# Strassen block products for 22 gate/up units of two feed-forward blocks

## The chip, the cores and the metric

The kernel runs on one core of one Trainium2 chip. It is timed in microseconds (us) of device time from start to end. Before the change three runs took 1771.74, 1771.89 and 1772.28 us; the median is 1771.89.

## What is computed

Three transformer-like blocks over 512 tokens and a model width of 1024 run one after the other: convolution mixer and feed-forward, dilated attention and feed-forward, and a third block with retention, sparse attention and a feed-forward with a small convolution. The change touches the first two feed-forwards and the additions around them:

```
def rmsnorm(x, g):
    y = x * rsqrt(mean(x * x, axis=-1) + EPS)
    return y * g

def swiglu(h, w_gate, w_up, w_down):
    return (silu(h @ w_gate) * (h @ w_up)) @ w_down      # 1024 -> 2816 -> 1024

h = rmsnorm(x, norm_ffn[i])
x = x + swiglu(h, ffn_w_gate[i], ffn_w_up[i], ffn_w_down[i])
```

## The kernel before

Everything is stored with channels on the 128 partitions and the 512 tokens as columns. A 1024-wide tensor is 8 such tiles. Weights come in **units**: a unit holds the weights of 256 output columns (two halves of 128) for all its input tiles, one half for the gate and one for the up projection in a gate/up unit. `LAYERS` (L24) lists the layers with their number of units and of input tiles: `pw2` 4 units of 8 tiles, `gu0a` 11 of 8, `dn0a` 4 of 11, `gu0b`, `dn0b`, `qkv` 9 of 8, `wo` 4 of 6, and for the second feed-forward `gu1a`, `dn1a`, `gu1b`, `dn1b`.

Each float32 product is made as three matmuls of rounded parts: weight high part by data high part, high by low, low by high (`product`, L640 to L648). A plain gate/up unit is therefore 2 halves x 8 tiles x 3 = 48 matmuls of 128x512. Weights arrive in `W_raw` (two buffers, SyncE's queue), ScalarE rounds them to `W_hi` (`split_hi`, `hi_of`, L1280 to L1294), and VectorE subtracts to get `W_lo` (`split_lo`, `lo_of`, L2059 to L2071). All three have two buffers, used in turn: the parts of unit u+2 can be written only when unit u is done (`acc_ready`), and unit u+2 can't begin before `w_lo` says that they are there (`unit`, L669).

Each engine has its own program, written out in order; nothing is rearranged by a scheduler. VectorE's part in a gate/up unit is `gate_steps` (L2221): scale both sums by the reciprocal root mean square R, multiply by the activated gate, then make the `W_lo` of the unit after next, then the low part of the hidden tile. In `pw2`, `wo` and the down layers it is `add_steps` (L2193): add the sums to X, make the normed low parts `H_lo` where a norm follows, then `W_lo`. ScalarE's programs of the same names (L1489, L1527) make `W_hi`, then `H_hi` and the squares for the norm. `R` enters only after the products, since it is a factor of each token.

Of the kernel before, what the change touches and what calls it, by code (L numbers as in the profile page):

```python
# [5 lines left out]
F32 = mybir.dt.float32  # L6
# [4 lines left out]
P = 128  # L11
# [17 lines left out]
          ("gu2a", 11, 8), ("dn2a", 4, 11), ("gu2b", 11, 8), ("dn2b", 4, 11)]  # L29

# [159 lines left out]
def build(nc, a, out):  # L190
# [6 lines left out]
    kts = [l.kt for l in order for _ in range(l.n)]  # L197
# [6 lines left out]
    with ctx:  # L204
# [25 lines left out]
        R = sb("R", [P, SEQ])  # L230
        STD = sb("STD", [P, SEQ])
# [17 lines left out]

        PADDED = SEQ + CONV_WIDTH - 1 + 2  # L250
# [17 lines left out]
        PT1 = [sb(f"PT1{i}", [P, SEQ], at=w_at + 11264 * i + 8192) for i in range(6)]  # L268
# [72 lines left out]
        ident, ones, swap, dup, dupswap, headsum = (cmat[:, i, :] for i in range(6))  # L341
        sel = [cmat[0:GROUP_HEADS, 6 + i, :] for i in range(2)]
        later = cmat[:, 8, :]
# [191 lines left out]
        std2_made = sem("std2_made")  # L535

# [8 lines left out]
        def _(sp):  # L545
            def load(L, src, j):
                u = j.plus(L.base)
                b = u.parity
                if u.i is not None or u.c >= 2:

                    sp.wait_ge(w_lo, u.v(1, -1))
# [39 lines left out]
            for k, L in enumerate(order):  # L591
# [30 lines left out]
                steps(sp, L.n, lambda j: load(L, a[L.name], j))  # L622
# [12 lines left out]
        def _(pe):  # L635
# [4 lines left out]
            def product(b, kt, half, k, x_hi, x_lo, bank=None, first=0, last=None):  # L640

                dst = PS[2 * b + half if bank is None else bank]
                last = kt - 1 if last is None else last
                c = k * COLS + half * P
                wh, wl = W_hi[b][:, c:c + P], W_lo[b][:, c:c + P]
# [4 lines left out]
            def products(b, kt, half, x_hi, x_lo, between=None):  # L650

                for k in range(kt):
                    last = product(b, kt, half, k, x_hi, x_lo)
                    if between is not None and k % 2 and k < kt - 1:
# [5 lines left out]
            def both_halves(b, kt, x_hi, x_lo, ready):  # L660

                for k in range(kt):
                    pe.wait_ge(*ready(k))
                    for half in range(2):
                        last = product(b, kt, half, k, x_hi, x_lo)
                        if k == kt - 1:
                            last.then_inc(acc_ready, 1)

            def unit(L, j, x_hi, x_lo, ready=None, between=None, beside_second=None):  # L669
# [4 lines left out]
                if ready is not None:  # L674
                    both_halves(u.parity, L.kt, x_hi, x_lo, ready)
                    return
                products(u.parity, L.kt, 0, x_hi, x_lo, between)
                products(u.parity, L.kt, 1, x_hi, x_lo, between or beside_second)
# [60 lines left out]
            def last_unit(L):  # L739
# [4 lines left out]
                for q in range(2):  # L744
                    if q:
                        pe.wait_ge(acc_free, u)
                    for half in range(2):
                        dst = PS[2 * ((u + q) % 2) + half][:, part(q)]
                        for k in range(L.kt):
                            c = k * COLS + half * P  # L750
                            wh, wl = W_hi[u % 2][:, c:c + P], W_lo[u % 2][:, c:c + P]
# [2134 lines left out]
```

## Time and profile before

| | |
|---|---|
| median of 3 runs | 1771.89 us |
| span of the profiled execution, first to last instruction | 1771.1 us |
| mean granted TensorE clock | 0.996 |
| TensorE matmuls busy | 1743.0 us, 98% |
| VectorE busy | 992.9 us, 56% |
| ScalarE busy | 713.7 us, 40% |
| GpSimd busy | 273.0 us, 15% |

For the profiled execution the page gives its span alone; what lies around the span of a run is about 0.8 us if the execution was like the median. Busy times of one group of matmuls can add up to more than the time that passed, because matmuls are pipelined: the start of one to the start of the next is the number that counts. `idle before` is time in which the engine had nothing to do before an instruction, with what released it.

### The profile page before, as it was taken

How to read it: one execution, taken by the hardware profiler on the slowest of the kernel's cores; microseconds unless marked ns; L12 is line 12 of the kernel's file. 1: busy time of each engine (PE TensorE's matmuls, PEld its weight loads, DVE VectorE, ACT ScalarE, POOL GpSimd, SP SyncE). 2: the span in 40 equal slices, each digit the busy share in tenths (PEclk: the TensorE clock that was granted, in tenths of full speed). 3: DMA queues.
4: the chain of work that ended last, by engine and by line, in shares of the span. 5: the costliest groups of instructions: out<-in, count | busy, mean ns of one | idle time of the engine just before them, and what ended most of it. 6: DMA issues, size and time to landing. Idle time of an engine off the chain costs nothing.

```text
span 1771.1 us, 21509 instructions
## 1 busy us (share of the span) xinstructions
PE 1743.0 (98%) x8282; PEld 1395.6 (79%) x8282; DVE 992.9 (56%) x1260; ACT 713.7 (40%) x1058; POOL 273.0 (15%) x207
## 2 busy tenths in 40 slices
PE   9999999999999999999999999999999999999997
PEld 6885888888888777888888888766677778888887
DVE  6997554424444555654424434559735687437753
ACT  6876332212232343432212233465664444314432
POOL 2993200000001000200000004572201200000002
PEclk9999999999999999999999999999999999999999
DMA  5210432222232311222222232523212223322221
GB/s 186 96 51 31 125 112 104 101 79 91 105 115 72 127 60 42 93 112 102 104 75 93 101 124 83 150 75 111 67 48 72 71 71 107 119 72 95 104 98 48
DMA packets 28918, 163.35 MB, mean 92 GB/s; under 512 B 4607, under 2 KB 7819, under 8 KB 12460
## 3 DMA queue, kind: packets, MB, share of 16 engines
q1 hardware_dynamic: 25664, 156.28, 25.4%
q10 hardware_dynamic: 3180, 6.07, 1.1%
q8 instruction: 48, 0.79, 0.2%
q14 instruction: 26, 0.21, 0.0%
HBM read 154.98 MB, written 4.47 MB: 90 GB/s over the span
## 4 chain that ended last, share of the span: by engine, by line
PE 83%; DVE 7%; POOL 6%; ACT 2%; issue 1%; DMA 0%; POOLq 0%; ACTq 0%; DVEq 0%
PE PS L646 26%; PE PS L648 25%; PE PS L647 25%; POOL CV L1939 4%; DVE W_lo L2071 1%; ACT W_hi L1294 1%; POOL ISC L2003 1%; PE PS L1113 1%; PE PS L1092 1%; PE PS L1104 0%; DVE WK L2494 0%; PE PS L943 0%; PE PS L977 0%; DVE TOP L2492 0%; DVE H_lo L2051 0%
## 5 line engine op out<-in xcount | busy, mean ns | idle before, releaser
L646 PE MATMUL PS<-H_hi,W_hi 128*128 128x512 f32 x1600 | 638.5, 399 | 7.3 <-DVE W_lo L2071 2.0
L648 PE MATMUL PS<-H_hi,W_lo 128*128 128x512 f32 x1600 | 624.1, 390 | 0.0
L647 PE MATMUL PS<-H_lo,W_hi 128*128 128x512 f32 x1600 | 623.9, 390 | 0.0
L1294 ACT ACTIVATE W_hi<-W_raw 128x2048 fp32r<-128x2048 f32 (+2 forms) x130 | 262.7, 2021 | 673.1 <-PE PS L648 673.1
L646 PEld LDWEIGHTS PS<-H_hi,W_hi 128*128 128x128 f32 x1600 | 300.8, 188 | 91.5 <-issue 23.0
L2071 DVE TENSOR_TENSOR W_lo<-W_raw,W_hi 128x2048 fp32r<-128x2048 f32 (+2 forms) x130 | 334.1, 2570 | 60.4 <-ACT W_hi L1294 60.0
L648 PEld LDWEIGHTS PS<-H_hi,W_lo 128*128 128x128 f32 x1600 | 300.6, 188 | 63.7
L647 PEld LDWEIGHTS PS<-H_lo,W_hi 128*128 128x128 f32 x1600 | 301.1, 188 | 58.5 <-issue 1.0
L1891 POOL TENSOR_TENSOR SSUM<-SSUM,SQ 128x512 f32<-128x512 f32 x43 | 63.3, 1472 | 1330.6 <-ACT SQ L1337 1328.9
L646 PE MATMUL PS<-HID_hi,W_hi 128*128 128x512 f32 x618 | 240.9, 390 | 1.5 <-DVE HID_lo L2190 1.4
L647 PE MATMUL PS<-HID_lo,W_hi 128*128 128x512 f32 x618 | 240.4, 389 | 0.0
L648 PE MATMUL PS<-HID_hi,W_lo 128*128 128x512 f32 x618 | 240.4, 389 | 0.0
L646 PEld LDWEIGHTS PS<-HID_hi,W_hi 128*128 128x128 f32 x618 | 116.0, 188 | 27.0 <-issue 2.5
L648 PEld LDWEIGHTS PS<-HID_hi,W_lo 128*128 128x128 f32 x618 | 116.0, 188 | 24.1
L647 PEld LDWEIGHTS PS<-HID_lo,W_hi 128*128 128x128 f32 x618 | 116.0, 188 | 24.0
L2232 DVE TENSOR_TENSOR T_u<-PS,R 128x512 f32<-128x512 f32 x44 | 30.4, 691 | 155.3 <-PE PS L648 155.3
L2240 DVE TENSOR_TENSOR T_hid<-T_u,T_act 128x512 f32<-128x512 f32 x66 | 45.7, 692 | 81.2 <-ACT T_act L1535 78.6
L2205 DVE TENSOR_TENSOR X<-X,PS 128x512 f32<-128x512 f32 x40 | 27.0, 684 | 113.9 <-PE PS L648 113.7
L2131 DVE SCALAR_TENSOR_TENSOR PS<-U,vecs,PS 128x512 f32<-128x512 f32 x112 | 74.7, 746 | 0.0
L1543 ACT ACTIVATE HID_hi<-T_hid 128x512 f32 (+1 forms) x66 | 41.8, 633 | 57.7 <-DVE T_hid L2240 57.7
L2051 DVE SCALAR_TENSOR_TENSOR H_lo<-X,vecs,H_hi 128x512 fp32r<-128x512 f32 x32 | 30.6, 956 | 27.4 <-ACT H_hi L1322 27.3
L2246 DVE TENSOR_TENSOR HID_lo<-T_hid,HID_hi 128x512 f32 (+1 forms) x66 | 45.2, 684 | 1.4 <-ACT HID_hi L1543 1.4
(344 smaller groups left out, 1571.1 us busy)
## 6 DMA issues: line engine op xcount, KB each, us to landing
W_raw<-in_inp SPq DMA_DIRECT2D x13, 1024.0 KB, 4.9
W_raw<-in_pw SPq DMA_DIRECT2D x11, 1024.0 KB, 4.8
W_raw<-in_gu0a SPq DMA_DIRECT2D x11, 1024.0 KB, 4.9
W_raw<-in_gu0b SPq DMA_DIRECT2D x11, 1024.0 KB, 4.8
W_raw<-in_gu1a SPq DMA_DIRECT2D x11, 1024.0 KB, 4.8
W_raw<-in_gu1b SPq DMA_DIRECT2D x11, 1024.0 KB, 4.9
W_raw<-in_gu2a SPq DMA_DIRECT2D x11, 1024.0 KB, 4.8
W_raw<-in_gu2b SPq DMA_DIRECT2D x11, 1024.0 KB, 4.9
```

The costliest lines, as they stand in the source:

```text
L646: nc.tensor.matmul(dst[:], wh, x_hi[:, k, :], start=(k == first), stop=False)
L647: nc.tensor.matmul(dst[:], wh, x_lo[:, k, :], start=False, stop=False)
L648: return nc.tensor.matmul(dst[:], wl, x_hi[:, k, :], start=False, stop=(k == last))
L1294: nc.scalar.activation(W_hi[b][:, 0:n], W_raw[b][:, 0:n], ACT.Copy).then_inc(w_hi, 1)
L1543: nc.scalar.activation(dst, T_hid[:], ACT.Copy).then_inc(hid_hi_made, 1)
L1891: nc.gpsimd.tensor_tensor(SSUM[:], SSUM[:], SQ[:, m.parity, :], ALU.add).then_inc(ss_made, 1)
L1939: nc.gpsimd.tensor_tensor(acc, acc, TAP[k % len(TAP)], ALU.add).then_inc(pool_tap, 1)
L2051: nc.vector.scalar_tensor_tensor(out=dst, in0=src, scalar=scale, in1=hi, op0=ALU.mult, op1=ALU.subtract).then_inc(h_lo_made, 1)
L2071: nc.vector.tensor_tensor(W_lo[b][:, 0:n], W_raw[b][:, 0:n], W_hi[b][:, 0:n].bitcast(F32), ALU.subtract).then_inc(w_lo, 1)
L2131: i = nc.vector.scalar_tensor_tensor(out=dst, in0=src, scalar=w, in1=acc, op0=ALU.mult, op1=ALU.add)
L2240: nc.vector.tensor_tensor(T_hid[:], T_u[:], T_act[:], ALU.mult).then_inc(hid_made, 1)
L2246: nc.vector.tensor_tensor(HID_lo[:, k, :].rearrange("p o n -> p (o n)"), T_hid[:], hi, ALU.subtract).then_inc(hid_lo_made, 1)
```

## The change

`KINDS` names for each of the four gate/up layers which units stay plain (P) and which are made by block products (S): 5, 6, 5 and 6 of 11. For an S unit the 1024 inputs are taken as 512 pairs (even and odd tiles), the output columns as gate and up, the tokens as two halves of 256. That is a 2x2 by 2x2 block product, made with seven products instead of eight. Each of the seven is 4 tiles x 3 matmuls of 128x256: 84 matmuls for an S unit. Four sums or differences of weight blocks are made by VectorE for each S unit (`first_sums`, `other_sums`), four of the data blocks once for a whole feed-forward (`EZ`, made in `pair_steps` beside `pw2` and `wo`). The weight parts of three of the seven go to three further buffers (`SLOT`). Products that share a destination are added up in PSUM, ScalarE takes partial sums out in between, and VectorE adds the rest. The factor R of the up projection is moved behind the down projection: there each of the 32 sums is multiplied by R and then added to X, two instructions in place of one. The `T_u` of a plain unit is copied out by ScalarE.

```
+KINDS = {"gu0a": "PPPSSPSSPSP", "gu0b": "PPSSPSSPSSP", "gu1a": "PPPSSPSSPSP", "gu1b": "PPSSPSSPSSP"}
...
+            def block_product(L, b, i, k, first, last):
...
+                nc.tensor.matmul(dst, wh, xh, start=start, stop=False, skip_group_check=True)
+                nc.tensor.matmul(dst, wh, xl, start=False, stop=False, skip_group_check=True)
+                return nc.tensor.matmul(dst, wl, xh, start=False, stop=last, skip_group_check=True)
+            def block_unit(L, j, l):
...
+                for i in range(PARTS):
+                    if i == 3:
+                        pe.wait_ge(part_taken, TAKEN0 + 4 * s + 1)
+                    if i == 4:
+                        pe.wait_ge(part_taken, TAKEN0 + 4 * s + 2)
+                        pe.wait_ge(slot_lo, SLOT0 + 3 * s + 1)
+                    if i == 5:
+                        pe.wait_ge(part_taken, TAKEN0 + 4 * s + 3)
+                        pe.wait_ge(slot_lo, SLOT0 + 3 * s + 2)
...
```

ScalarE beside `pw2` and `wo` (`add_steps` replaced by):

```
+            def pair_steps(name, norm, gain, l):
+                L = layers[name]
+                for j in range(L.n):
+                    if j < L.n - 2:
+                        split_hi(act, L, At(j))
+                    for m in (2 * j, 2 * j + 1):
+                        h_hi(norm, gain, At(m))
+                        square(norm, At(m))
+                    if j:
+                        pair(j - 1, l)
+                    if j < L.n - 1:
+                        even(norm, gain, j, l)
+                for j in (L.n - 2, L.n - 1):
+                    split_hi(act, L, At(j))
+                even(norm, gain, L.n - 1, l)
```

VectorE there, and in the gate/up layers:

```
+            def pair_steps(name, x0, norm, gain, l, bias=None):
+                L = layers[name]
+                for j in range(L.n):
+                    u = L.base + j
+                    if j:
+                        differences(norm, gain, j - 1, l)
... (two additions to X, acc_free)
+                    for half in range(2):
+                        h_lo(norm, gain, At(2 * j + half))
+                    if j:
+                        pair(j - 1, l)
+                    if j < L.n - 2:
+                        split_lo(L, At(j))
+                for j in (L.n - 2, L.n - 1):
+                    split_lo(L, At(j))
...
+                    if last == "S":
+                        up(j - 1)
+                        if this == "S":
+                            slots_of(u)
+                    if j:
+                        hid(j - 1)
+                    if then == "S":
+                        first_sums(u + 1)
+                    if j:
+                        hid_lo(j - 1)
+                    if then == "S":
+                        front_of(u + 1)
+                        other_sums(u + 1)
+                        front_sums(u + 1)
+                    elif j and not second:
+                        weights(j + 1)
...
+                    gate(j)
+                    if this == "P" and then == "S":
+                        slots_of(u + 1)
```

In the order of the instructions three places show it. VectorE at the handover from `pw2` to `gu0a`, before: from the additions of `pw2`'s third unit on. `W_lo_56` in the fourth row belongs to the first unit of `gu0a`, `W_lo_57` to the second.

```order
L2207 SCALAR_TENSOR_TENSOR X<-PS,vecs,X 128x512 [waits acc_ready] x2
L2051 SCALAR_TENSOR_TENSOR H_lo<-X,vecs,H_hi 128x512 [waits x_ready,h_hi_made]
L2051 SCALAR_TENSOR_TENSOR H_lo<-X,vecs,H_hi 128x512 [waits h_hi_made]
L2071 TENSOR_TENSOR W_lo_56<-W_raw_52,W_hi_54 128x2048 [waits w_hi]
L2207 SCALAR_TENSOR_TENSOR X<-PS,vecs,X 128x512 [waits acc_ready] x2
```

And now, from the additions of the fourth unit on:

```order
L2563 SCALAR_TENSOR_TENSOR X<-PS,vecs,X 128x512 [waits acc_ready] x2
L2304 SCALAR_TENSOR_TENSOR H_lo<-X,vecs,H_hi 128x512 [waits x_ready,h_hi_made]
L2304 SCALAR_TENSOR_TENSOR H_lo<-X,vecs,H_hi 128x512 [waits h_hi_made]
L2547 TENSOR_TENSOR E_lo_98<-EZ_102,E_hi_94 128x1024 [waits diag_made]
L2324 TENSOR_TENSOR W_lo_56<-W_raw_52,W_hi_54 128x2048 [waits w_hi]
L2324 TENSOR_TENSOR W_lo_57<-W_raw_53,W_hi_55 128x2048 [waits w_hi]
```

The `W_lo_56` of the first gate/up unit stood ahead of the additions of the fourth unit, and now stands behind them.

ScalarE at the same place before, from the second `H_hi` of the second unit on:

```order
L1322 ACTIVATE H_hi<-X,vecs 128x512 [waits x_ready]
L1337 ACTIVATE SQ<-X 128x512 [waits ss_made]
L1294 ACTIVATE W_hi_54<-W_raw_52 128x2048 [waits acc_ready,raw_in0]
L1322 ACTIVATE H_hi<-X,vecs 128x512 [waits x_ready]
L1337 ACTIVATE SQ<-X 128x512 [waits ss_made]
```

And now, from the second `H_hi` of the fourth unit on:

```order
L1490 ACTIVATE H_hi<-X,vecs 128x512 [waits x_ready]
L1505 ACTIVATE SQ<-X 128x512 [waits ss_made]
L1713 ACTIVATE E_hi_94<-EZ_102 128x1024 [waits conv_made]
L1438 ACTIVATE W_hi_54<-W_raw_52 128x2048 [waits acc_ready,raw_in0]
L1438 ACTIVATE W_hi_55<-W_raw_53 128x2048 [waits acc_ready,raw_in1]
```

`W_hi_54`, the high part for the first gate/up unit, was ahead of the third unit's `H_hi` before and is behind the fourth unit's now, and behind `E_hi`. The same order stands between `wo` and `gu1a`.

VectorE in a gate/up unit before (the first of `gu0a`; the others have no `RECIPROCAL`):

```order
L2056 RECIPROCAL R<-STD 128x512 [waits std_made]
L2230 TENSOR_TENSOR T_g<-PS,R 128x512 [waits acc_ready,r_made]
L2232 TENSOR_TENSOR T_u<-PS,R 128x512 [waits acc_ready]
L2240 TENSOR_TENSOR T_hid<-T_u,T_act 128x512 [waits gate_act,acc_free]
L2071 TENSOR_TENSOR W_lo_56<-W_raw_52,W_hi_54 128x2048 [waits w_hi]
L2246 TENSOR_TENSOR HID_lo<-T_hid,HID_hi 128x512 [waits hid_hi_made]
```

In a plain unit between two S units (the sixth of `gu0a`) now; `SUM` and `W_sum` are the summed weight blocks, `SLOT` the three extra buffers:

```order
L2602 TENSOR_TENSOR T_u<-T_u,PS 128x256 [waits xc_sq]
L2605 TENSOR_TENSOR T_u<-T_u,PS 128x256 [waits xc_made,acc_ready]
L2611 TENSOR_TENSOR T_hid<-T_u,T_act 128x512 [waits acc_free,gate_act]
L2336 TENSOR_TENSOR W_sum_58<-W_raw_52 128x512 [waits acc_ready,raw_in0]
L2338 TENSOR_TENSOR W_sum_58<-W_sum_58,W_raw_52 128x512 [waits ln_sum]
L2616 TENSOR_TENSOR HID_lo<-T_hid,HID_hi 128x512 [waits hid_hi_made]
L2352 TENSOR_TENSOR W_lo_56<-W_raw_52,W_hi_54 128x1024 [waits ln_act,hid_lo_made]
L2345 TENSOR_TENSOR SUM_70<-W_raw_52,W_sum_58 128x512 [waits ln_sum]
L2346 TENSOR_TENSOR SUM_72<-W_raw_52 128x512
L2359 TENSOR_TENSOR W_lo_56<-W_sum_58,W_hi_54 128x1024 [waits ln_sum,w_hi]
L2587 TENSOR_TENSOR T_g<-PS,R 128x512 [waits acc_ready]
L2367 TENSOR_TENSOR SLOT_lo_67<-SUM_70,SLOT_hi_64 128x512 [waits ln_hi_made]
```

Two more `SLOT_lo` rows follow. Five instructions have become fourteen, and the one `W_lo` of 128x2048 two of 128x1024 with sums between them.

## Rows read from the trace of the kernel before

**Rows 1.** The page: busy time, and the chain that ended last.
```profile
PE 1743.0 (98%) x8282; PEld 1395.6 (79%) x8282; DVE 992.9 (56%) x1260; ACT 713.7 (40%) x1058; POOL 273.0 (15%) x207
PE 83%; DVE 7%; POOL 6%; ACT 2%; issue 1%; DMA 0%; POOLq 0%; ACTq 0%; DVEq 0%
```

**Rows 2.** Waits of TensorE, 200 to 810 us: total, times, longest.
```profile
PE PS L929 <- DVE VQK L2264: 0.8, 1, 0.8
...
PE PS L646 <- DVE W_lo L2071: 0.3, 1, 0.3
```

**Rows 3.** VectorE in `gu0a`, timeline: start, duration, instruction, idle before.
```profile
244.54 0.69 DVE L2232 TENSOR_TENSOR T_u<-PS,R 128x512 f32<-128x512 f32 x1 [4.55 <-PE PS L648]
247.00 0.69 DVE L2240 TENSOR_TENSOR T_hid<-T_u,T_act 128x512 f32<-128x512 f32 x1 [1.78 <-ACT T_act L1535]
247.62 2.28 DVE L2071 TENSOR_TENSOR W_lo<-W_raw,W_hi 128x2048 fp32r<-128x2048 f32 x1
249.82 0.68 DVE L2246 TENSOR_TENSOR HID_lo<-T_hid,HID_hi 128x512 f32 x1
...
255.42 0.69 DVE L2232 TENSOR_TENSOR T_u<-PS,R 128x512 f32<-128x512 f32 x1 [3.80 <-PE PS L648]
```

**Rows 4.** TensorE in the last unit, timeline: 128x256 products.
```profile
1741.35 0.28 PE L752 MATMUL PS<-HID_hi,W_hi 128*128 128x256 f32 x1
...
1751.30 0.28 PE L754 MATMUL PS<-HID_hi,W_lo 128*128 128x256 f32 x1
1751.42 0.50 PE L771 MATMUL PS<-cmat,SSUM 128*128 128x1 f32 x4
```

**Rows 5.** Groups by line and shape: busy us, mean ns, idle before.
```profile
L2754 DVE TENSOR_TENSOR X<-X,PS 128x256 f32<-128x256 f32 x12 | 5.0, 420 | 0.4
L2662 DVE TENSOR_TENSOR W_lo<-W_raw,W_hi 128x1024 fp32r<-128x1024 f32 x2 | 2.4, 1219 | 0.0
L1695 ACT ACTIVATE PT<-PS 128x256 f32<-128x256 f32 x8 | 3.0, 380 | 7.2 <-PE PS L1104 7.1
```

**Rows 6.** Handover from `pw2` to `gu0a`: timelines of TensorE, VectorE and ScalarE.
```profile
210.34 0.39 PE L646 MATMUL PS<-H_hi,W_hi 128*128 128x512 f32 x1
...
204.66 3.37 DVE L2071 TENSOR_TENSOR W_lo<-W_raw,W_hi 128x2048 fp32r<-128x2048 f32 x1
210.54 0.75 DVE L2207 SCALAR_TENSOR_TENSOR X<-PS,vecs,X 128x512 f32<-128x512 f32 x1 [1.85 <-PE PS L648]
...
210.60 1.92 ACT L1294 ACTIVATE W_hi<-W_raw 128x2048 fp32r<-128x2048 f32 x1 [6.69 <-PE PS L648]
212.43 0.70 ACT L1322 ACTIVATE H_hi<-X,vecs 128x512 fp32r<-128x512 f32 x1
213.03 0.62 ACT L1337 ACTIVATE SQ<-X 128x512 f32<-128x512 f32 x1
213.56 0.71 ACT L1322 ACTIVATE H_hi<-X,vecs 128x512 fp32r<-128x512 f32 x1
```

**Rows 7.** `wo` and its handover to `gu1a`: timelines of VectorE and TensorE.
```profile
725.99 0.69 DVE L2205 TENSOR_TENSOR X<-X,PS 128x512 f32<-128x512 f32 x1 [0.72 <-PE PS L648]
730.56 2.86 DVE L2071 TENSOR_TENSOR W_lo<-W_raw,W_hi 128x1536 fp32r<-128x1536 f32 x1
...
742.58 0.50 PE L646 MATMUL PS<-H_hi,W_hi 128*128 128x512 f32 x1 [0.31 <-DVE W_lo L2071]
```

**Rows 8.** TensorE, the kernel's first microseconds, timeline.
```profile
1.39 6.11 PE L704 MATMUL PS<-ZERO 128*128 128x512 f32 x8 [1.39 <-POOL ZERO L1881]
8.58 1.10 PE L704 MATMUL PS<-ZERO 128*128 128x512 f32 x2
```

**Rows 9.** Stretches at the end: TensorE, its loads, VectorE, ScalarE, GpSimd busy; granted clock; DMA.
```profile
1763.00:1764.00 1.00, 0.09 (x1) 0.00 (x0) 0.97 (x3) 0.38 (x1) 0.41 (x1) 1.00 0.07 24
1764.00:1765.00 1.00, 0.00 (x0) 0.00 (x0) 0.93 (x4) 0.00 (x0) 0.92 (x2) 0.56 0.39 131
1765.00:1766.00 1.00, 0.00 (x0) 0.00 (x0) 0.96 (x3) 0.00 (x0) 0.92 (x3) 0.50 0.39 131
```

More of the change, by code:

```diff
@@ L230, in build @@
         R = sb("R", [P, SEQ])
+        std_at = top[0]
         STD = sb("STD", [P, SEQ])
@@ L648, in product, with products @@
                 return nc.tensor.matmul(dst[:], wl, x_hi[:, k, :], start=False, stop=(k == last))
[L650 to L654, printed above, removed]
+            def products(b, L, half, x_hi, x_lo, between=None):
+                for k in range(L.kt):
+                    last = product(b, L, half, k, x_hi, x_lo)
+                    if between is not None and k % 2 and k < L.kt - 1:
                         between()
@@ L825, in _ @@
                 for half in range(2):
-                    last = product(0, L.kt, half, k, H_hi, H_lo)
+                    last = product(0, L, half, k, H_hi, H_lo)
                     if k == L.kt - 1:
@@ L834, in _ @@
                     for k in range(L.kt):
-                        last = product(j % 2, L.kt, half, k, H_hi, H_lo)
+                        last = product(j % 2, L, half, k, H_hi, H_lo)
                         if k == L.kt - 1:
@@ L872, in three_units @@
                         for half in range(2):
-                            last = product(L.base % 2, L.kt, half, k, H_hi, H_lo)
+                            last = product(L.base % 2, L, half, k, H_hi, H_lo)
                             if k == L.kt - 1:
@@ L876, in three_units @@
                     if k:
-                        last = product(1 - L.base % 2, L.kt, 0, k - 1, H_hi, H_lo)
+                        last = product(1 - L.base % 2, L, 0, k - 1, H_hi, H_lo)
                         if k == L.kt:
@@ L880, in three_units @@
                 for k in range(L.kt):
-                    last = product(1 - L.base % 2, L.kt, 1, k, H_hi, H_lo)
+                    last = product(1 - L.base % 2, L, 1, k, H_hi, H_lo)
                     if k == L.kt - 1:
@@ L892, in three_units @@
                     for k in range(L.kt):
-                        last = product(L.base % 2, L.kt, half, k, H_hi, H_lo, 6 + half)
+                        last = product(L.base % 2, L, half, k, H_hi, H_lo, 6 + half)
                         if k == L.kt - 1:
@@ new lines, in mixed @@
+            def mixed(l, name, norm=None):
+                L = layers[name]
+                for j in range(L.n):
+                    if kind(L, j) == "S":
+                        block_unit(L, j, l)
+                    else:
+                        unit(L, At(j), H_hi, H_lo, after(h_lo_made, H_BASE[norm]) if norm is not None and j == 0 else None)
+                    if norm is not None and j == 0:
+                        rms_sum(norm)
+            def feed_forward(l, norm):
+                if f"gu{l}a" in KINDS:
+                    mixed(l, f"gu{l}a", norm)
+                    linear(f"dn{l}a", HID_hi, HID_lo, ready=after(hid_lo_made, gu_base[f"gu{l}a"]))
+                    mixed(l, f"gu{l}b")
+                    linear(f"dn{l}b", HID_hi, HID_lo, ready=after(hid_lo_made, gu_base[f"gu{l}b"]))
+                    return
@@ L1030, in _ @@
                     for k in range(L.kt):
-                        last = product(u % 2, L.kt, half, k, H_hi, H_lo, QKV_BANKS[j] + half)
+                        last = product(u % 2, L, half, k, H_hi, H_lo, QKV_BANKS[j] + half)
                         if k == L.kt - 1:
@@ L1048, in _ @@
                 for half in range(2):
-                    last = product(L.base % 2, L.kt, half, k, HID_hi, HID_lo)
+                    last = product(L.base % 2, L, half, k, HID_hi, HID_lo)
                     if k == L.kt - 1:
@@ L1247, in _ @@
                     for k in range(L.kt):
-                        last = product(u % 2, L.kt, half, k, H_hi, H_lo, INP_BANKS[j][half])
+                        last = product(u % 2, L, half, k, H_hi, H_lo, INP_BANKS[j][half])
                         if k == L.kt - 1:
@@ L1262, in _ @@
                 for half in range(2):
-                    last = product(L.base % 2, L.kt, half, k, H_hi, H_lo, first=4, last=3)
+                    last = product(L.base % 2, L, half, k, H_hi, H_lo, first=4, last=3)
                     if k == 3:
```

440 lines of the change are left out of this document (352 added, 88 removed).

## The prediction, made before the changed kernel ran

> **What bounds the kernel now.** I read the page first: TensorE's matmuls are busy for 98% of the span and the chain that ended last lies on TensorE for 83% [rows 1]. The chain runs through long stretches of matmuls, so what counts there is the time from the start of one matmul to the next, and every gap. The waits of TensorE come next: from 200 to 810 us, which holds both feed-forwards and the attention up to near their end, the longest is 0.8 us, and the only one on weights is 0.3 us, just at the handover from `wo` to `gu1a` [rows 2, 7]. So this part is bound by the number and size of matmuls and nothing hides a new gap. VectorE has 56% [rows 1], but not evenly: in a plain gate/up unit it idles 4.55 and 3.80 us before `T_u` and 1.78 us before `T_hid` [rows 3].
>
> **The gain on TensorE.** Two `T_u` in a row start at 244.54 and 255.42 us: a plain unit of 48 matmuls lasts 10.88 us, 0.227 us for one [rows 3]. The last unit of the kernel has the very shape that an S unit uses, 128x256 with new weights each time. Its 84 first matmuls (66 of the first token half, 18 of the second up to the column sums) go from 1741.35 to 1751.42 us: 10.07 us, 0.120 us for one [rows 4]. An S unit also has 84. It saves 10.88 - 10.07 = 0.81 us, and 22 of them 17.8 us. Half the columns cost 53% of the time, so the saving is 7% of a unit and not an eighth.
>
> The Trainium skill (TensorE: Matmul & The Clock Gate, section "Wait — 56ns, not 53.3ns?") gives columns divided by 2.4 GHz plus about 2.5 ns for one matmul. By that a plain unit takes 48 x 0.2158 = 10.36 us, an S unit 84 x 0.1092 = 9.17 us, and the saving is 26.2 us. Here the trace disagrees: above 512 / 2.4 and 256 / 2.4 both rows leave about 13 ns for each matmul, so the rows decide.
>
> **The handover from `pw2` to `gu0a`.** Here I put the largest cost. TensorE began `gu0a` at 210.34 us without a wait, because the `W_lo` of its first unit had been started at 204.66 [rows 6]. Now ScalarE rounds that unit's weights only behind the last `H_hi`, its square and the high part of a data pair, and VectorE's `W_lo` follows. All of this hangs on the last addition to X, which can't start before the last `pw2` unit is done: 210.54 us [rows 6]. From there: addition 0.75, to 211.3. `H_hi`, the next instruction after 0.61: 211.9. Square, the next after 0.53 (213.03 to 213.56): 212.5. `E_hi`, 128x1024 on ScalarE, has no row: between `W_hi` of 2048 with 1.92 us and `H_hi` of 512 with 0.70 us [rows 6]; half way by size gives about 1.0: 213.5. `W_hi` 1.92: 215.4. `W_lo` 2.28 when GpSimd is quiet [rows 3], with 0.1 for each signal: 217.8. TensorE restarts at 217.8 instead of 210.34: **7.5 us**. If GpSimd's last addition of squares overlaps it, `W_lo` takes up to 3.37 [rows 6], 8.6. The new low bound is the chain without `E_hi`, 6.5. `H_lo` for this unit is ready by then, so it is no second wait. The second unit's split has all of the first unit as cover.
>
> **The handover from `wo` to `gu1a`.** A `wo` unit has 36 matmuls, 8.16 us, and the same VectorE work in it, so VectorE falls behind. The end of the second unit lets X start at 725.99. `W_lo` for the fourth unit started at 730.56 and took 2.86 [rows 7]. Now `E_lo` (128x1024, 1.22 us [rows 5]) stands ahead of it and waits until ScalarE has made `E_hi` at about 730.9: `W_lo` runs from 732.1 to between 733.9 and 735, where TensorE wants it at 734.1. Then four differences of 128x256 (0.42 each [rows 5], two of them waiting for the one before: 1.7 to 1.9), two additions, and ScalarE's `H_hi`, square, `E_hi`, `ZB` with the next `E_lo` and four differences lead to the last two additions; the last starts at 742.7 to 743.9. From its start to TensorE is 7.3 us as above: 750.0 to 751.2. TensorE began at 742.58 before [rows 7]. The delay is 7.4 to 8.6, I take **8.0 us**.
>
> **The clock behind these two gaps.** No gap of this length lies inside the kernel before. At its end TensorE's last matmul runs into the stretch from 1763, the granted clock is 0.56 in the stretch from 1764 and 0.50 from 1765: the lower level, 1.2 GHz [rows 9]. So it should fall in a gap of 7 to 8 us, and the first matmuls behind it run at half speed. The nearest price is the kernel's start, where four float32 products (two records each) take 6.11 us, and one later takes 1.10 [rows 8]: 6.11 - 4 x 1.10 = 1.7 us lost at least, half of 6.11 at most, 3.1. I take 2.2 each, **4.4 us**; the other end is nothing, if the clock stays up.
>
> **Waits inside the S units.** VectorE's instructions of 128x512 start 0.61 apart (247.00 to 247.62), those of 2048 2.20 [rows 3]; 1024 takes 1.22 and 256 takes 0.42 [rows 5], about 1.14 and 0.35 apart. A plain unit between two S units costs VectorE 2 x 0.35 + 10 x 0.61 + 2 x 1.14 = 9.1 us with the three `SLOT_lo`, near 9.8 with its waits on its own results, of 10.88. That fits, hardly. What is late first is in the second S unit of a pair. Counted from its start, the gate's activation of the unit before ends near 1.6 when VectorE comes from a full step; three `SLOT_hi` 0.54 apart go to 3.2, `SLOT_lo` to 4.2, `T_hid` to 4.9, `HID_hi` to 5.5, the second take of a partial sum (0.38 [rows 5]) to 5.9 where the fifth product wants it at 4 x 1.44 = 5.76. Behind it stands `W_hi` with 1.83, and the third take ends at 8.1 where the sixth product wants it at 7.2. So up to 1 us for a pair that starts late, nothing for one that doesn't. There are 10 pairs: 0 to 10 us. The worst is the first pair of `gu0a` and `gu1a`, where the `RECIPROCAL` and the last four differences come before. I take 2 us for each of these two layers, **4 us** in all. Queued behind a late take are the takes and activations of the same unit; VectorE's `gate` waits for them and TensorE only through the next unit's `free` and weights, one unit later.
>
> **At nothing.** The multiplication by R behind the down projection adds 32 instructions of 0.61 to VectorE; a down unit lasts 66 x 0.227 = 15 us, and the next weights are done in it. Where the norm follows, ScalarE is still busy with a `W_hi` of 1.92 when X is ready, so 0.8 more on X hides behind that. `T_u` of a plain unit moves to ScalarE, 40% busy. SyncE's loads keep their order, and wait for the last `SLOT_lo` of the unit two back instead of `W_lo`, some 2 to 4 us into a unit; over 5 us remain for a transfer of 5. The differences beside `pw2` find 10.88 us for about 8.6 of VectorE work.
>
> **Sum.** Span 1771.1 - 17.8 + 7.5 + 8.0 + 4.4 + 4.0 = 1777.2; with the 0.8 us around it 1778.0, where the median before is 1771.89: slower by 0.34%. With all unknown costs at their lower ends (6.5, 7.4, 0, 0) it is 1768.0, with all at their upper (8.6, 8.6, 6.2, 10) 1787.5.
>
> **The rivals.**
> - *The gaps are there, their company isn't.* The clock stays up and ScalarE and VectorE are never late: 1771.9 - 17.8 + 7.5 + 8.0 = 1769.6, slower and faster parts cancel. For it: VectorE's step fits in a unit by the sum. Against it: the clock at the end of the kernel, and the tight takes. The page's rule on the matmul would bring the sum to 1778.0 - 8.4 = 1769.6 as well; the rows on both shapes speak against that.
> - *Faster: the handovers cost little.* If ScalarE reached the first gate/up unit's weights early, or TensorE had other work there, only the saving and small waits stay: 1771.9 - 17.8 + 4 = 1758. For it speaks only that VectorE and ScalarE have idle time in `pw2`; against it the order of the instructions, in which nothing can pass.
> - *VectorE becomes the bound.* From about 10% on its instructions, which overfills the 9.8 of 10.88 us, its lateness isn't made up in the plain units: each of the 10 pairs costs 1.5 us or so, 15 in place of 4: 1789. For it: instructions of VectorE have taken half as long again beside GpSimd (2.28 against 3.37). Against it: GpSimd has no work within the gate/up layers.
>
> **How the numbers follow.** The forecast has a chance of 0.62, no company for the gaps 0.21 (the matmul rule 0.03 of it), cheap handovers 0.08, VectorE as the bound 0.09. A difference under 0.2%, 3.5 us, can't be told from none. The first rival falls within it, as does the forecast's lower edge below 1775.4 (0.08 of its 0.62), against a little of the first rival that comes out below 1768.3 (0.02). VectorE's rival is slower. So faster 0.10, same 0.27, slower 0.63. The range goes from 1768.5 to 1786: it leaves out the cheap handovers and the far side of VectorE as the bound.
>
> **What would show it.** In the profile of the changed kernel: 128x256 matmuls 0.120 us apart, and an S unit of 10.1 us; TensorE waiting for `W_lo` (L2324) twice, 7 to 9 us each; a granted clock of 0.5 at the end of each of these gaps and some microseconds beyond; waits of TensorE on ScalarE's takes (`T_g`, `T_u`), up to a microsecond each, mainly in the first pair of `gu0a` and `gu1a`. The prediction is wrong if the first unit of `gu0a` starts without a gap, if the distance of matmuls is not 0.120, or if the waits on takes or on `W_lo` within the layers sum to much more than 4 us.

## The result, and the profile after

| | before | changed |
|---|---|---|
| median of the runs | 1772.09 us (4 runs, 1771.74 to 1773.0) | 1780.12 us (4 runs: 1775.23, 1779.88, 1780.37, 1781.77) |
| ratio, 95% interval | | 1.004 [1.0025, 1.0054] |
| span of the profiled execution | 1771.1 us | 1773.4 us (the run of 1775.23 us) |

The changed kernel is slower, as forecast (1778.0 us, 1768.5 to 1786). In every run of either kernel that lists both, the time is about 1.8 us above its span, not 0.8. Three of the four runs are 4.7 to 6.5 us above the profiled one; the fifth experiment looks for the reason. Four single runs in the later sets, at 2176 to 9830 us, were disturbed and are left out.

The page of the changed kernel, the lines of [rows 1], with VectorE's and ScalarE's added work:

```profile
PE 1729.9 (98%) x9074; PEld 1421.6 (80%) x9074; DVE 1143.6 (64%) x1576; ACT 806.1 (45%) x1296; POOL 273.2 (15%) x207
PE 83%; DVE 7%; POOL 6%; ACT 2%; issue 2%; DMA 0%; POOLq 0%; ACTq 0%; DVEq 0%
```

TensorE has 13 us less matmul time, and still the span is 2.3 us longer. The waits of TensorE in the whole changed kernel name the place (total, times, longest):

```profile
PE PS L732 <- DVE W_lo L2324: 18.5, 4, 9.2
```

Before, waits on `W_lo` were 2.0 us in two pieces, and one of 1.7 us is still there. TensorE's timeline (start, duration, instruction, idle before) shows both handovers; 210.53 is the last matmul of `pw2`, 743.07 that of `wo`:

```profile
210.53 0.39 PE L734 MATMUL PS<-HID_hi,W_lo 128*128 128x512 f32 x1
218.11 0.79 PE L732 MATMUL PS<-H_hi,W_hi 128*128 128x512 f32 x1 [7.19 <-DVE W_lo L2324]
218.70 0.63 PE L733 MATMUL PS<-H_lo,W_hi 128*128 128x512 f32 x1
219.13 0.63 PE L734 MATMUL PS<-H_hi,W_lo 128*128 128x512 f32 x1
...
222.12 0.40 PE L732 MATMUL PS<-H_hi,W_hi 128*128 128x512 f32 x1
222.35 0.39 PE L733 MATMUL PS<-H_lo,W_hi 128*128 128x512 f32 x1
...
743.07 0.39 PE L734 MATMUL PS<-HID_hi,W_lo 128*128 128x512 f32 x1
752.61 0.79 PE L732 MATMUL PS<-H_hi,W_hi 128*128 128x512 f32 x1 [9.16 <-DVE W_lo L2324]
```

Before, the first of them ran without a stop [rows 6] and the second with 0.31 us [rows 7]. Read the distance of starts behind a gap, too: 0.43 (218.70 to 219.13) where it is 0.23 from 222.12 on. The stretches of 1 us (columns as in [rows 9]) tell why:

```profile
214.00:215.00 1.00, 0.00 (x0) 0.00 (x0) 1.00 (x1) 1.00 (x1) 0.40 (x1) 1.00 0.00 0
215.00:216.00 1.00, 0.00 (x0) 0.00 (x0) 0.72 (x2) 1.00 (x2) 0.00 (x0) 0.65 0.00 0
216.00:217.00 1.00, 0.00 (x0) 0.00 (x0) 1.00 (x1) 1.00 (x1) 0.00 (x0) 0.50 0.00 0
...
221.00:222.00 1.00, 1.00 (x4) 0.81 (x3) 0.00 (x0) 0.00 (x0) 0.00 (x0) 0.50 1.01 410
222.00:223.00 1.00, 1.00 (x5) 0.78 (x5) 0.00 (x0) 0.00 (x0) 0.00 (x0) 0.94 0.97 393
```

The granted clock goes to 0.50, the 1.2 GHz level, while TensorE idles, and is back only after some 4 us of matmuls. Nine matmuls start from 218.11 until the tenth at 222.12, 4.01 us for 9 x 0.227 = 2.04: 2.0 us lost. Behind the second gap the low level lasts until just before 758, some 12 matmuls: 2.6 us.

What stands in the first gap, in the timelines of VectorE and ScalarE:

```profile
210.96 0.75 DVE L2563 SCALAR_TENSOR_TENSOR X<-PS,vecs,X 128x512 f32<-128x512 f32 x1 [2.12 <-PE PS L734]
211.75 0.72 ACT L1490 ACTIVATE H_hi<-X,vecs 128x512 fp32r<-128x512 f32 x1 [1.62 <-DVE X L2563]
212.37 0.61 ACT L1505 ACTIVATE SQ<-X 128x512 f32<-128x512 f32 x1
212.89 1.04 ACT L1713 ACTIVATE E_hi<-EZ 128x1024 fp32r<-128x1024 f32 x1
213.84 3.69 ACT L1438 ACTIVATE W_hi<-W_raw 128x2048 fp32r<-128x2048 f32 x2
215.76 4.49 DVE L2324 TENSOR_TENSOR W_lo<-W_raw,W_hi 128x2048 fp32r<-128x2048 f32 x2 [0.28 <-ACT W_hi L1438]
```

This is the chain as the prediction laid it out, step for step: addition, `H_hi`, square, `E_hi` (estimated 1.0, measured 1.04), `W_hi`, `W_lo`. It begins at 210.96 and lets TensorE go at 218.11, 7.15 us; 7.3 was predicted.

At `wo` the gap is longer than predicted. VectorE there, with the row of GpSimd that lies beside it last:

```profile
740.59 2.09 DVE L2547 TENSOR_TENSOR E_lo<-EZ,E_hi 128x1024 fp32r<-128x1024 f32 x1
...
744.25 1.28 DVE L2561 TENSOR_TENSOR X<-X,PS 128x512 f32<-128x512 f32 x2
...
750.27 4.48 DVE L2324 TENSOR_TENSOR W_lo<-W_raw,W_hi 128x2048 fp32r<-128x2048 f32 x2
...
738.55 3.05 POOL L2144 TENSOR_TENSOR SSUM<-SSUM,SQ 128x512 f32<-128x512 f32 x2 [6.35 <-ACT SQ L1505]
```

`E_lo` takes 2.09 us instead of 1.22, and VectorE has no idle time from there to the last additions to X, which begin at 744.25, the second of them near 744.9. I had worked out 743.9 at the latest (744.3 on this clock, since this profile runs 0.4 us later from its start). They also come as a pair, so that both `H_hi` and both squares stand in the chain: from the second addition it is 7.7 us to TensorE. With the 0.51 us that TensorE waits for a `W_lo` at 735.00, `gu1a` starts 9.6 us later against `gu0b`'s end than before (241.31 us in place of 231.68).

The S units do on TensorE just what was worked out. In the first of them (timeline), the 128x256 matmuls start 0.12 apart:

```profile
253.41 0.39 PE L734 MATMUL PS<-H_hi,W_lo 128*128 128x512 f32 x1
253.63 0.28 PE L1001 MATMUL PS<-H_hi,W_hi 128*128 128x256 f32 x1
253.75 0.28 PE L1002 MATMUL PS<-H_lo,W_hi 128*128 128x256 f32 x1
```

`gu0b`, from its first matmul to the first of `dn0b`, went from 119.68 us (391.22 to 510.90) to 114.82 (396.48 to 511.30): 4.86 for six S units, 0.81 each. `gu1b` shows the same two lengths. The stretch within `gu0a` shows VectorE at 84.17 of 118 us, and TensorE without a hole:

```profile
228.00:346.00 118.00, 118.00 (x718) 105.88 (x717) 84.17 (x112) 56.38 (x84) 0.00 (x0) 1.00 0.29 104
```

**The ledger of the span.** From 1771.1: the first matmul stages come 0.4 us later from the start; first gap +7.35 (the wait and the step over a matmul); low clock behind it +2.0; the move at `wo` +9.6; low clock behind that +2.6; 22 S units -17.8; what is left, -1.9 (about 0.5 in each of `gu0a` and `gu1a` beside the S units, 0.9 behind the feed-forwards). Sum 1773.4, the measured span. The 0.9 can't be put down to the change: the stretch from `dn1b`'s end to the next feed-forward's hidden tiles takes 413.8 us in the profile before, 412.9 in this one and 414.7 in another profile of the same changed kernel (experiment 5). So the ledger closes for this pair of profiles, and a sum for a typical run is good to about 1 us.

### The profile page after: what moved, and what is told of

It is laid out like the page before. It is cut to its first block, busy times and chain, and to the rows that moved or that the text cites. A ratio compares the mean times of both kernels' runs of the same rounds, so it can differ in the third digit from the quotient of the medians.

```text
span 1773.4 us, 23112 instructions
## 1 busy us (share of the span) xinstructions
PE 1729.9 (98%) x9074; PEld 1421.6 (80%) x9074; DVE 1143.6 (64%) x1576; ACT 806.1 (45%) x1296; POOL 273.2 (15%) x207
## 4 chain that ended last, share of the span: by engine, by line
PE 83%; DVE 7%; POOL 6%; ACT 2%; issue 2%; DMA 0%; POOLq 0%; ACTq 0%; DVEq 0%
PE PS L732 21%; PE PS L734 21%; PE PS L733 21%; POOL CV L2192 4%; PE PS L1001 4%; PE PS L1002 4%; PE PS L1003 4%; DVE W_lo L2324 1%; POOL ISC L2256 1%; ACT W_hi L1438 1%; DVE WK L2918 1%; PE PS L1237 1%; PE PS L1258 0%; PE PS L1249 0%; PE PS L1088 0%
## 5 line engine op out<-in xcount | busy, mean ns | idle before, releaser
L732 PE MATMUL PS<-H_hi,W_hi 128*128 128x512 f32 x1248 | 503.2, 403 | 22.2 <-DVE W_lo L2324 18.0
L734 PE MATMUL PS<-H_hi,W_lo 128*128 128x512 f32 x1248 | 488.5, 391 | 0.0
L733 PE MATMUL PS<-H_lo,W_hi 128*128 128x512 f32 x1248 | 488.2, 391 | 0.0
L1438 ACT ACTIVATE W_hi<-W_raw 128x2048 fp32r<-128x2048 f32 (+1 forms) x108 | 204.6, 1896 | 355.0 <-PE PS L734 355.0
L2324 DVE TENSOR_TENSOR W_lo<-W_raw,W_hi 128x2048 fp32r<-128x2048 f32 (+1 forms) x108 | 258.1, 2391 | 86.8 <-ACT W_hi L1438 57.2
L732 PEld LDWEIGHTS PS<-H_hi,W_hi 128*128 128x128 f32 x1248 | 235.6, 189 | 91.4 <-issue 21.7
L734 PEld LDWEIGHTS PS<-H_hi,W_lo 128*128 128x128 f32 x1248 | 235.2, 188 | 50.8
L733 PEld LDWEIGHTS PS<-H_lo,W_hi 128*128 128x128 f32 x1248 | 235.7, 189 | 45.2 <-issue 1.2
L732 PE MATMUL PS<-HID_hi,W_hi_tail 128*128 128x512 f32 x138 | 53.7, 389 | 0.0
L733 PE MATMUL PS<-HID_lo,W_hi_tail 128*128 128x512 f32 x138 | 53.7, 389 | 0.0
```

Source lines behind the costliest of these rows:

```text
L732: nc.tensor.matmul(dst[:], wh, x_hi[:, k, :], start=(k == first), stop=False)
L733: nc.tensor.matmul(dst[:], wh, x_lo[:, k, :], start=False, stop=False)
L734: return nc.tensor.matmul(dst[:], wl, x_hi[:, k, :], start=False, stop=(k == last))
L1438: i = nc.scalar.activation(W_hi[b][:, 0:n], W_raw[b][:, 0:n], ACT.Copy)
L2324: i = nc.vector.tensor_tensor(W_lo[b][:, 0:n], W_raw[b][:, 0:n], W_hi[b][:, 0:n].bitcast(F32), ALU.subtract)
```

## The experiments

**1. Splits early.** The one edit: in `pw2` and `wo` every unit's weight split goes back to its old place.

```
 # pair_steps, ScalarE and, in the same way, split_lo on VectorE ahead of pair()
-                    if j < L.n - 2:
-                        split_hi(act, L, At(j))
+                    split_hi(act, L, At(j))
...
-                for j in (L.n - 2, L.n - 1):
-                    split_hi(act, L, At(j))
```

> The changed kernel, but in pw2 and wo the weights of the unit after next are split in every step where they were before the change (ScalarE ahead of the two H_hi, VectorE behind the two H_lo and ahead of the data pair); the Strassen units stay. Theory A (the two handovers eat the gain): both gaps before gu0a and gu1a go, at most 1.5 us is left at gu1a because VectorE is full in wo, the clock stays at 1.00, and the time is 1772.1 - 17.8 + 1 to 3 = 1755 to 1758 us, with a narrow spread of runs. Theory B (the S units cost more than their matmuls, by waits or by contention, and the gaps are a side matter): 1765 us or more.

Measured: 1755.72 us (1754.42 to 1755.87, 4 runs), ratio to before 0.9904 [0.9889, 0.9919]. TensorE in its timeline passes from `pw2` to `gu0a` without a gap:

```profile
210.38 0.39 PE L734 MATMUL PS<-HID_hi,W_lo 128*128 128x512 f32 x1
210.61 0.39 PE L732 MATMUL PS<-H_hi,W_hi 128*128 128x512 f32 x1
```

Before `gu1a` 1.2 us are left. So the place of the splits in two layers makes a kernel that is 17 us faster than before into one that is slower. It beats both kernels. On VectorE this edit also moves the other splits of the two layers ahead of the pair work; experiment 4 moves the last two alone.

**2. Plain units.** All of the change, but no S unit: `KINDS` is "P" * 11 for the four layers.

> The changed kernel with all 44 units of the four layers plain, so that the late weight splits, the data pairs and the moved factor R stay and the Strassen units go. Theory A: the changed kernel's 1780.1 plus 22 x 0.81 = 1798 us (1793 if the run is like the profiled one), gaps of 7.2 and 9.2 us before gu0a and gu1a as in the changed kernel. Theory B (S units cost more than they save): under 1790 us.

Measured: 1793.77 us (1792.23 to 1794.8, 4 runs), ratio 1.0123 [1.0107, 1.0138]. Its waits of TensorE are those of the changed kernel:

```profile
PE PS L732 <- DVE W_lo L2324: 18.6, 4, 9.2
```

So none of these waits comes from the S units; they come with `pair_steps`, and experiments 1 and 4 show that it is its order. The spans of the two profiles, 1790.4 and 1773.4, differ by 17.0 us, near the 17.8 of the S units. All four runs lie near 1793, which was expected only for runs like the profiled one; none shows the 5 us on top that three of four runs of the changed kernel have.

**3. Gap filled.** In each gap TensorE gets matmuls of 128x512 on a constant, whose result nobody uses: 7 products of two records each ahead of `gu0a`, 9 ahead of `gu1a`. The waits stay as long, only TensorE is busy in them.

```
+                    if norm is not None and j == 0:
+                        idle_products(AUX[1], 9 if l else 7)
```

> The changed kernel with idle matmuls (7 before gu0a, 9 before gu1a, about 0.94 us each, into an unused bank) in the two gaps; everything else waits as before. Theory A with the clock as its part: the gaps stay 7.4 and 9.2 us long, the granted clock stays 1.00, nothing is lost behind them, and the time falls by what the low clock costs: to 1770 to 1771 us for every run, with a spread under 1 us where the changed kernel has 1775 to 1782. Rival (the spread and the 5 us of the slower runs have another cause, such as waits within the S units that come and go): 1775 to 1778 with the spread still there.

Measured: 1770.76 us (1770.33 to 1772.02, 11 runs), ratio 0.9991 [0.9982, 1.0]. TensorE's timeline: the filling, and then matmuls 0.33 and soon 0.23 apart; the start at 217.94 is nearly the 218.11 of the changed kernel:

```profile
210.58 6.17 PE L806 MATMUL PS<-cmat 128*128 128x512 f32 x14
217.94 0.50 PE L732 MATMUL PS<-H_hi,W_hi 128*128 128x512 f32 x1 [1.19 <-DVE W_lo L2326]
218.27 0.40 PE L733 MATMUL PS<-H_lo,W_hi 128*128 128x512 f32 x1
```

The stretches of the same microseconds as above have the clock at 1.00:

```profile
215.00:216.00 1.00, 1.00 (x4) 0.45 (x3) 0.72 (x2) 1.00 (x2) 0.00 (x0) 1.00 0.00 0
216.00:217.00 1.00, 0.75 (x2) 0.00 (x0) 1.00 (x1) 1.00 (x1) 0.00 (x0) 1.00 0.00 0
```

This is the first rival (gaps, but no company) as a kernel, and it comes out 1.2 us from where that rival was put, 1769.6, and within 0.2% of before. The clock is worth the rest. The runs spread over 1.7 us, where under 1 was expected.

**4. Late splits alone.** The kernel before, with only the splits of the last two units of `pw2` and `wo` moved behind the last `H_hi` and `H_lo`; no pairs, no R behind the down projection, no S unit.

```
+                    late = name in ("pw2", "wo")
+                    if not late or (j.i is None and j.c < L.n - 2):
                         split_hi(act, L, j)
...
+                    if late and j.c == L.n - 1:
+                        split_hi(act, L, At(L.n - 2))
+                        split_hi(act, L, At(L.n - 1))
```

> The kernel before the change with one thing moved: in pw2 and wo the splits of the last two steps come behind the last H_hi and H_lo, as in the changed kernel, without data pairs or Strassen units. Theory A: gaps of about 6.5 us at both handovers (the chain X, H_hi, square, W_hi, W_lo), and with 2 to 5 us of low clock behind each a time of 1772.1 + 13 + 4 to 10 = 1789 to 1795 us, with a spread of several us among the runs. Rival (the pair work makes the gaps, the place of the splits does little): under 1780 us.

Measured: 1789.21 us (1788.05 to 1789.86, 4 runs), ratio 1.0093 [1.0078, 1.0109], 16.5 us over before.

```profile
PE PS L646 <- DVE W_lo L2076: 14.1, 3, 6.2
```

Two gaps of 6.2 us, and 1.7 that was there before. 16.5 less 12.4 leaves 4.1 for the clock and small things. The gaps of the whole change are longer (7.2 and 9.2) by the pair work that stands in them.

**5. The changed kernel again,** on another chip, since three of four runs had been 5 us above the profiled one.

> The changed kernel once more, unedited, to see what goes with the spread of its runs (1775.2 to 1781.8 in four). Theory A: the time of a run follows its mean granted clock: the low clock behind the two gaps lasts 4 to 8 us each, runs lie between 1774 and 1782 us, and each 0.001 less of mean clock (3.5 us more at the lower level) goes with 1.8 us more. Rival: runs differ at the same clock.

Measured: 1777.21 us (11 runs), ratio 1.0025 [1.0016, 1.0034]. Nine runs lie at 1774.77 to 1778.31, two at 1779.98 and 1781.22. The profiled one is that of 1781.22, and its timeline differs from the other at the kernel's start:

```profile
1.38 5.13 PE L790 MATMUL PS<-ZERO 128*128 128x512 f32 x8 [1.38 <-POOL ZERO L2134]
8.03 1.03 PE L797 MATMUL PS<-cmat,SSUM 128*128 128x1 f32 x8 [1.52 <-DMA cmat<-in_cmat]
```

The first products were done 1.4 us sooner (5.13 against 6.51 us), and TensorE then waited 1.52 us for its constants, 0.21 in the other profile. Why they were done sooner no row shows: the granted clock stands at 1.00 in both there. Then, in stretches:

```profile
10.00:11.00 1.00, 1.00 (x10) 0.94 (x9) 0.26 (x1) 0.71 (x2) 0.00 (x0) 1.00 1.04 426
11.00:12.00 1.00, 1.00 (x2) 0.33 (x1) 0.44 (x1) 0.00 (x0) 0.00 (x0) 0.56 1.06 442
...
21.00:22.00 1.00, 1.00 (x3) 0.34 (x2) 1.00 (x2) 0.25 (x1) 0.00 (x0) 0.82 0.00 0
```

Ten microseconds at the low level, from about 11.1 to 21.4, with TensorE busy. `gu0a` begins at 222.72 in this run instead of 218.11, 4.6 us later, behind the same gap of 7.19 us. So this has nothing to do with the handovers, and kernels without them have such runs as well: two of the 21 runs of the kernel before beside experiments 8 to 10 took 1778.64 and 1778.98 us at a mean clock of 0.993 against 0.995 to 0.997. No trace of those two was kept, nor of the three slower runs of the recorded result; that they are the same event is likely from their times, not shown.

**6. Five S units in a row,** on top of experiment 1, to find where VectorE becomes the bound: `gu0b` and `gu1b` are "PPSSPSSSSSP", seven S units each in place of six, five of them in a row.

> The kernel with the early splits, and in gu0b and gu1b the pattern PPSSPSSSSSP: seven Strassen units instead of six, five of them in a row. Theory A (VectorE has its room in the plain units between pairs, and a Strassen unit between two others needs some 11 us of VectorE against 10.1 of TensorE): waits of 2 to 3 us in TensorE in each of the two layers, against 2 x 0.81 us saved, so 1755.7 - 1.6 + 5 = 1759 us. Rival (VectorE isn't near its limit): 1754.1 us and no waits.

Measured: 1755.18 us (four runs at 1754.84 to 1755.25, two at 1760.78 and 1761.53 with a mean clock of 0.993), ratio 0.9916 [0.9902, 0.9929]: the same as experiment 1. That is neither of the two expected times, 1759 and 1754.1. TensorE does wait for the takes now, but little where 2 to 3 us in each layer were expected (160 to 1100 us):

```profile
PE PS L1001 <- ACT T_g L1754: 0.8, 2, 0.4
```

`gu0b` lasts 115.06 us where six S units gave 114.82: the added unit's 0.81 went into about 1.05 us of lateness (115.06 - 114.82 + 0.81), most of it in steps too short to be listed as waits. `gu1b` lasts 115.07. VectorE is the bound there, as its timeline shows:

```profile
472.14 1.29 DVE L2364 TENSOR_TENSOR SLOT_lo<-SUM,SLOT_hi 128x512 fp32r<-128x512 f32 x2 [0.36 <-ACT SLOT_hi L1461]
...
482.78 1.29 DVE L2364 TENSOR_TENSOR SLOT_lo<-SUM,SLOT_hi 128x512 fp32r<-128x512 f32 x2 [0.36 <-ACT SLOT_hi L1461]
```

One S unit behind another takes 10.64 us of VectorE, with 0.36 idle, and 10.07 of TensorE, so each adds some 0.6 us of lateness. TensorE feels it first at 474.42 us, in the fourth of the five: three in a row ran without a stop.

**7. Short gap.** Two of the idle products in each gap instead of 7 and 9: the stretch without work is 5.5 us in place of 7.2.

> The changed kernel with two idle matmuls at the start of each of the two gaps, so that TensorE's idle stretch shrinks from 7.2 and 9.2 to about 5.4 and 7.3 us while all else waits as before. Theory A (the low clock is the only other cost of a gap, and it comes with idleness of this length): the clock still falls in both, the time stays within that of the changed kernel, 1774 to 1781 us. Rival (shorter gaps escape it): near 1770.8 us, as with the gaps filled.

Measured: 1775.06 us (1774.86 to 1776.24, and one of 1780.0; 11 runs), ratio 1.0018 [1.0009, 1.0027]. TensorE's timeline, and the stretch of 1 us around the fall:

```profile
210.76 1.88 PE L806 MATMUL PS<-cmat 128*128 128x512 f32 x4
218.12 0.79 PE L732 MATMUL PS<-H_hi,W_hi 128*128 128x512 f32 x1 [5.48 <-DVE W_lo L2326]
```

```profile
216.00:217.00 1.00, 0.00 (x0) 0.00 (x0) 1.00 (x1) 1.00 (x1) 0.00 (x0) 0.95 0.00 0
217.00:218.00 1.00, 0.00 (x0) 0.00 (x0) 1.00 (x2) 1.00 (x2) 0.00 (x0) 0.50 0.00 0
...
223.00:224.00 1.00, 1.00 (x4) 0.82 (x3) 0.00 (x0) 0.00 (x0) 0.00 (x0) 0.63 0.96 369
```

The clock fell all the same, only later, and came back later too: in this profile 13 matmuls run from 218.12 until the next at 223.79, where they would take 2.95 us at full clock, so 2.7 us are lost. The second gap, 7.42 us idle, costs 3.0. So a stretch of 5.5 us does not escape the low clock. Whether it costs less is not settled: this profile is one of the slower runs, and the median is 2.1 us under that of the changed kernel on the same chip (experiment 5), though the two intervals overlap.

**8. Plain units, splits early:** experiments 1 and 2 in one.

> The kernel with the early splits and all 44 units of the four layers plain: the data pairs and the moved factor R stay, the Strassen units and the late splits go. Theory A (each Strassen unit is worth 0.81 us and the rest of the change costs nothing once the splits are early): 1755.7 + 17.8 = 1773.5 us, within 1 us of the kernel before plus the 1.2 us wait at gu1a. Rival (the pair work or the two additions for R cost something on their own that the Strassen units' gain hides): the time differs from 1773.5 by 3 us or more.

Measured: 1772.34 us (1771.67 to 1773.89, 12 runs), ratio 0.9995 [0.9986, 1.0004]. So pairs, data differences and the multiplication by R behind the down projection cost nothing that the time shows, as predicted. Against experiment 1 the S units are worth 16.6 us by the medians and 18.2 by the profiled spans (1772.1 and 1753.9).

**9. Start covered.** The changed kernel with five `ZERO` products at the start instead of four, so that TensorE has work until the constants come.

```
-            zero_products(4)
+            zero_products(5)
```

> The changed kernel with five zero matmuls instead of four at the very start, in the time in which TensorE waits for the constants. Theory A (the runs near 1780 us are those in which the clock falls from 12 to 22 us, after a wait of 1.5 us for the constants between the start matmuls and the column sums): no run near 1780, all at 1774.5 to 1778.5 us, a mean clock of 0.990 or more in each. Rival (the slower runs come from the two gaps or the units): some runs at 1780 to 1782 with a clock of 0.988 stay.

Measured: 1776.4 us (1774.67 to 1777.28, 12 runs), ratio 1.002 [1.0011, 1.0028]. None of the 12 is near 1780. That fits the reading of the start, but doesn't prove it: with 2 in 11 of run 5, none in 12 happens one time in eleven. The profile adds to it:

```profile
1.39 6.49 PE L790 MATMUL PS<-ZERO 128*128 128x512 f32 x10 [1.39 <-POOL ZERO L2134]
```

Ten records take what eight took in the first profile, so these are the quicker products of run 5; the wait for the constants is 0.20 us here, and the clock stays at 1.00. Of the twelve profiles of this case, only run 5's has the fall, and it has the longest wait there (1.52 us; 1.18 in experiment 4 and 1.05 or less in the others).

**10. Both:** experiment 1 with five `ZERO` products.

> The kernel with the early splits, and the fifth zero matmul at the start: 1755 to 1756 us in every run, none 5 us above; nothing else is changed, so the median is that of the early splits.

Measured: 1755.69 us (1754.72, 1755.55, 1755.69, 1757.17, 1760.04), ratio 0.991 [0.9893, 0.9927]. One run at 1760.04 with a clock of 0.993: the extra product doesn't take the event away for certain, or the event has a second form. This stays open. Runs 9 and 10 had the same chip, and their difference is the price of the late splits: 20.7 us. Between experiments 2 and 8 it is 21.4.

## Why the prediction was right, step by step

The direction and the mechanism hold, and the sum was within 2.1 us of the recorded median (1780.12) and within 1.6 of the changed kernel with its start covered (1776.4). Some of that is luck. Two terms were off in opposite directions, and the recorded median holds about 5 us that no step had: with eleven runs on another chip the changed kernel is 4.6 us slower than before and not 8 (experiment 5), close to the 3.5 us that the prediction called too small to tell from none.

- **The gain on TensorE,** 22 x 0.81 = 17.8: exact in `gu0b` and `gu1b` (4.86 = 6 x 0.81). The rows on 128x256 of another unit [rows 4] were the right source. The formula of the Trainium skill (TensorE: Matmul & The Clock Gate, "Wait — 56ns, not 53.3ns?") would have made 1.19 us for an S unit's saving; measured are 0.81, and a distance of 0.120 us and not 0.109.
- **First handover,** 7.5: measured 7.35 on the path, with every step in its place.
- **Second handover,** 8.0, range 7.4 to 8.6: measured 9.6. This is a mis-sized step. `E_lo` was put down with the 1.22 us of a quiet stretch [rows 5], and I had applied GpSimd's presence to `W_lo` alone: 0.9 of the 1.6 us. Another 0.4 is the second `H_hi` and square in the chain, 7.7 us where I had 7.3; 0.3 is left that no row prices.
- **The clock behind the gaps,** 4.4: 4.6 in the profiled run, 5.6 by experiments 9 and 3 (1776.4 - 1770.8), 4.3 by experiments 7 and 3 with the shorter gaps. The size was right, the source was in part luck: in the profile before, the granted clock stands at 1.00 over the whole of the kernel's start [rows 8], so no row shows that those products ran at the low level.
- **Waits inside the S units,** 4.0: none in any of the 22. The failed step is "the gate's activation of the unit before ends near 1.6". In the first pair of `gu0a`, which I had called the worst, the second S unit begins at 263.7; ScalarE's rows there are these:

```profile
263.27 0.63 ACT L1739 ACTIVATE T_act<-T_g 128x512 f32<-128x512 f32 x1 [0.43 <-DVE T_g L2595]
...
267.62 0.36 ACT L1757 ACTIVATE T_u<-PS 128x256 f32<-128x256 f32 x1
267.88 1.90 ACT L1438 ACTIVATE W_hi<-W_raw 128x2048 fp32r<-128x2048 f32 x1
269.69 0.37 ACT L1757 ACTIVATE T_g<-PS 128x256 f32<-128x256 f32 x1
```

  The activation ends at 263.90, 0.2 us into the unit. All that hangs on it is early by the same amount: the second take ends at 267.98, 4.3 us into the unit and not 5.9, and the third at 270.06, 6.4 and not 8.1, where TensorE wants it at 7.2. VectorE was simply not behind when the pair began. Experiment 6 puts the margin: even five in a row cost only a microsecond.
- **What lies around the span,** 0.8: it is 1.8. The estimate took the profiled execution to be like the median, and nothing had shown that.
- **At nothing:** held, by experiment 8.

The terms as measured: 1771.1 - 17.8 + 7.35 + 9.6 + 4.6 + 0 + 0.4 - 1.9 = 1773.4, and 1.8 around it gives 1775.2. The other 5 us of the recorded median come most likely from the fall of the clock at the kernel's start, which cost 4.6 us in the profile of run 5; no step of the prediction had it.

**The rivals.** "The gaps are there, their company isn't" failed by the clock alone, since its other half, no waits on the takes, was true. "The handovers cost little" (1758) failed in this kernel and is experiment 1 (1755.7): with nothing but the order changed it comes true, so the price was in the order of instructions and not in the pair work. "VectorE becomes the bound" (1789) is refuted by the absence of waits; experiment 6 shows VectorE as the bound only in a longer row of S units.

## What to carry to other kernels

When a step that hands over to the next layer is rewritten, keep the preparation of the next layer's first weights ahead of the work that waits for this layer's last result; behind it, the whole chain from the last matmul becomes a gap on TensorE. Price such a gap with a surcharge for the clock (2 to 3 us each here for idle stretches of 5.5 to 9 us), and if it can't be removed, idle matmuls in it return the surcharge. Halving the columns of a matmul took 53% of the time here, so a block product that saves an eighth of the arithmetic saved 7%.

## What the runs showed of the hardware

- **VectorE beside GpSimd is blocked, not slowed.** I had read 3.37 us for `W_lo` instead of 2.28 as a slowdown by half. GpSimd's pair of additions ends at 738.55 + 3.05 = 741.60; `E_lo` starts at 740.59 and ends at 742.68, which is 1.1 us behind GpSimd's end, near its own 1.22. Had it run at half speed beside GpSimd, 0.5 us would have been lost, and 0.87 are. The earlier one, in `pw2`, fits too: GpSimd until 205.45, `E_lo` from 204.43 to 206.53:

```profile
204.43 2.10 DVE L2547 TENSOR_TENSOR E_lo<-EZ,E_hi 128x1024 fp32r<-128x1024 f32 x1
...
202.39 3.06 POOL L2144 TENSOR_TENSOR SSUM<-SSUM,SQ 128x512 f32<-128x512 f32 x2 [6.96 <-ACT SQ L1505]
```

  So does the 3.37 us itself, in the kernel before: `W_lo` starts at 204.66 and ends at 208.03 [rows 6], 2.1 us behind GpSimd's end at 205.89, near its own 2.28:

```profile
202.85 3.04 POOL L1891 TENSOR_TENSOR SSUM<-SSUM,SQ 128x512 f32<-128x512 f32 x2 [7.85 <-ACT SQ L1337]
```

  The Trainium skill (SBUF — State Buffer, "SBUF: two separate sides") says that the port pair of the two engines is an exclusive lock, held for the whole instruction, against VectorE operations with two inputs in SBUF while GpSimd's reads SBUF too. These rows agree. The cost is then what is left of GpSimd's instruction, whatever the size of VectorE's: about 0.9 here for an instruction of 1.22, and 1.1 for one of 2.28.
- **The clock can fall at the kernel's start under a busy TensorE.** In the profile of run 5 it was at 0.50 from about 11.1 to 21.4 us although TensorE shows as busy; what it ran before were products with a single column (128x1) between `ZERO` products, and before these it had waited 1.52 us. The other profiles have the same products, a shorter wait and no fall. Why it falls in some runs and not in others is not settled.
